# A two-layer attention block on one core: rotations, score products and VectorE's steps in another order

## What is computed

```python
proj = x @ w_in
a_in, b_in, c_in = jnp.split(proj, [A_COLS, A_COLS + B_COLS], axis=-1)
o_a = dilated_mixture(...)                       # 6 heads, kind "a"
o_b = diff_attention(bq[..., 0, :], bq[..., 1, :], bk[..., 0, :], bk[..., 1, :], bv, lam, ...)
                                                 # 4 heads, kind "b": a = probs(q1, k1) - lam * probs(q2, k2)
q = (rms_norm(c_q, ...) @ w_uq)                  # 6 heads, kind "c", from a latent
kv = (rms_norm(c_kv, ...) @ w_ukv)
q_c = concat([q[..., :C_NOPE], apply_rope(q[..., C_NOPE:])])
k_c = concat([kv[..., :C_NOPE], apply_rope(k_r)])
o_c = causal_attention(q_c, k_c, kv[..., C_NOPE:])
heads = jnp.concatenate([o_a, o_b, o_c], axis=-1)
h = layer_norm(DEEPNORM_ALPHA * x + heads @ w_o, ...)
```

## Time and profile before

| | us |
|---|---|
| median of 3 runs | 1985.44 (1985.15 to 1985.68) |
| the profiled execution | 1987.52 |
| its span, first to last instruction | 1985.6 |
| attention steps of the first of the two layers | about 841.8 to 937.4 |
| attention steps of the second | 628.6 later, about 1470.5 to 1566.0 |

### The profile page before, as it was taken

How to read it: one execution, slowest core, us unless ns; L and a number is a source line. 1 busy time by engine, 2 the same in 40 slices (tenths; PEclk the granted TensorE clock), 3 DMA queues, 4 the chain that set the end, 5 groups by cost and what they waited for, 6 DMA issues and landing times.

```text
span 1985.6 us, 26901 instructions
## 1 busy us (share of the span) xinstructions
PE 1934.6 (97%) x10454; PEld 1636.5 (82%) x10454; DVE 797.2 (40%) x1819; ACT 833.3 (42%) x1586; POOL 701.1 (35%) x553
## 2 busy tenths in 40 slices
PE   8999999999999999999999999999999999999997
PEld 4898889877789888877888888888887898888886
DVE  3665557442556435476511111017367551111003
ACT  3321268355237546577233232115477533232222
POOL 0523312125450335310544454445321245454542
PEclk9999999999999999999999999999999999999999
DMA  9544311112330124310333333222420123333321
GB/s 276 163 165 155 127 55 44 33 43 85 106 128 22 57 64 130 89 54 22 85 98 93 106 86 127 95 89 85 128 80 23 59 70 106 105 86 106 113 100 43
DMA packets 198261, 183.72 MB, mean 93 GB/s; under 512 B 31702, under 2 KB 166220, under 8 KB 198136
## 3 DMA queue, kind: packets, MB, share of 16 engines
q1 hardware_dynamic: 192104, 170.67, 27.9%
q10 hardware_dynamic: 6032, 11.33, 1.8%
HBM read 179.86 MB, written 5.40 MB: 93 GB/s over the span
## 4 chain that ended last, share of the span: by engine, by line
PE 86%; DVE 5%; ACT 3%; issue 2%; POOL 2%; DMA 1%; SPq 0%; DVEq 0%; ACTq 0%
PE ps L1330 23%; PE ps L1332 23%; PE ps L1331 23%; PE ps L1423 3%; PE ps L1918 2%; PE ps L1841 2%; POOL w_lo L731 2%; PE ps L1390 2%; PE ps L1409 2%; PE ps L1936 1%; PE ps L1453 1%; ACT w_hi L786 1%; PE ps L1368 1%; DVE sc L2498 1%; PE ps L1351 1%
## 5 line engine op out<-in xcount | busy, mean ns | idle before, releaser
L731 POOL TENSOR_TENSOR w_lo<-raw,w_hi 128x512 fp32r<-128x512 f32 (+1 forms) x518 | 679.2, 1343 | 1183.0 <-ACT w_hi L786 1182.9
L786 ACT ACTIVATE w_hi<-raw 128x1024 fp32r<-128x1024 f32 (+2 forms) x261 | 258.6, 1037 | 269.2 <-PE ps L1332 204.5
L1330 PE MATMUL ps<-g_hi,w_lo 128*128 128x512 f32 (+1 forms) x928 | 348.4, 375 | 1.4 <-POOL w_lo L731 1.4
L1331 PE MATMUL ps<-g_lo,w_hi 128*128 128x512 f32 (+1 forms) x928 | 347.5, 374 | 0.0
L1332 PE MATMUL ps<-g_hi,w_hi 128*128 128x512 f32 (+1 forms) x928 | 347.5, 374 | 0.0
L1330 PEld LDWEIGHTS ps<-g_hi,w_lo 128*128 128x128 f32 x928 | 174.7, 188 | 33.8 <-issue 1.7
L1331 PEld LDWEIGHTS ps<-g_lo,w_hi 128*128 128x128 f32 x928 | 174.7, 188 | 31.2
L1332 PEld LDWEIGHTS ps<-g_hi,w_hi 128*128 128x128 f32 x928 | 174.7, 188 | 30.9
L1330 PE MATMUL ps<-h_hi,w_lo 128*128 128x512 f32 (+1 forms) x496 | 180.1, 363 | 2.5 <-POOL w_lo L731 1.6
L2636 DVE TENSOR_TENSOR tmp_f<-ps,tmp_f 128x512 f32<-128x512 f32 x44 | 30.4, 692 | 370.7 <-PE ps L1332 370.7
L1331 PE MATMUL ps<-h_lo,w_hi 128*128 128x512 f32 (+1 forms) x496 | 174.6, 352 | 0.0
(11 more groups left out here) (293 smaller groups left out, 3469.3 us busy)
## 6 DMA issues: line engine op xcount, KB each, us to landing
raw<-in_w_in SPq DMA_DIRECT2D x30, 1024.0 KB, 5.1
raw<-in_w_mod SPq DMA_DIRECT2D x24, 1024.0 KB, 6.3
raw<-in_w_gate SPq DMA_DIRECT2D x44, 512.0 KB, 3.9
raw<-in_w_up SPq DMA_DIRECT2D x44, 512.0 KB, 5.1
raw<-in_w_down SPq DMA_DIRECT2D x22, 1024.0 KB, 4.8
raw<-in_w_out SPq DMA_DIRECT2D x8, 1024.0 KB, 5.0
strips<-bias_rows ACTq DMA_DIRECT2D x18, 256.0 KB, 3.5
raw<-in_w_in SPq DMA_DIRECT2D x16, 256.0 KB, 4.4
```

What stands on the lines that cost most here:

```text
L731: pool.tensor_tensor(w_lo[:, i % SPLIT, a:e], raw_of(what)[:, a:e], w_hi[:, i % SPLIT, a:e].bitcast(F32), ALU.subtract).then_inc(s_tile_lo ...
L786: act.activation(w_hi[:, i % SPLIT, a:b], raw_of(what)[:, a:b], ACT.Copy).then_inc(s_tile_hi.sem, s_tile_hi.nth((what, n)))
L1330: pe.matmul(o, lhs[1], rhs[0], start=first, stop=False)
L1331: pe.matmul(o, lhs[0], rhs[1], start=False, stop=False)
```

## The change

PE: the first rotation now stands behind the second key product instead of behind all three, the second behind the third. Scores 8 and 9 stand before the value products and not behind them. Score 10 stays behind them.

ACT: exp2(8) and exp2(9) come first, then the copies of the first three value products, then the copy of turn 0, then the copy of the fourth value product.

DVE: in each step the output rows come first, then the pair, then the scores, where it was scores, pair, rows.

The banks of the scores are shifted by one place, so that scores 8 and 9 go into banks 0 and 4, and the buffers are counted from unit 8, so that these two lie over the query weights, which are used up by then.

```diff
--- before.py
+++ after.py
@@ -602,7 +602,7 @@
             return u, ranks
 
         N_S, N_T, N_B, N_P = 3, 5, 5, 3
-        S_BANKS, T_BANKS = (0, 4, 6), (2, 1, 3, 5, 7)
+        S_BANKS, T_BANKS = (4, 6, 0), (2, 1, 3, 5, 7)
         UNITS, RANKS = units2()
         STEPS = len(UNITS) + N_B - 1
         FROM = N_B
@@ -610,7 +610,7 @@
 
         def probs_of(i):
 
-            return strips[:, B_HEADS + EARLY_AT[i], :] if i < EARLY else sc2[i % N_B]
+            return strips[:, B_HEADS + EARLY_AT[i], :] if i < EARLY else sc2[(i - EARLY) % N_B]
 
         LAST = len(RANKS) - 1
 
@@ -1232,9 +1232,15 @@
                         act.wait_ge(s_mm.sem, s_mm.at((y, what, c)))
                         for g in range(2):
                             act.activation(dst[0:HD, 2 * c + g, :], ps[HD * g:HD * g + HD, CB[what][c], :], ACT.Copy, scale=scale).then_inc(s_proj.sem, s_proj.nth((y, what, c, g)))
-                act.wait_ge(s_mm.sem, s_mm.at((y, "vc", XT - 1)))
-                for t in range(XT):
+                def vc_out(t):
+
+                    act.wait_ge(s_mm.sem, s_mm.at((y, "vc", t)))
                     act.activation(vc[:, t, :], ps[:, VCB[t], 0:384], ACT.Copy).then_inc(s_proj.sem, s_proj.nth((y, "vc", t)))
+
+                exp2(EARLY)
+                exp2(EARLY + 1)
+                for t in range(XT - 1):
+                    vc_out(t)
                 for step in range(FROM, STEPS):
                     r = turns(step)
                     if r is not None:
@@ -1243,7 +1249,9 @@
                         if r >= N_P:
                             act.wait_ge(s_mixed.sem, s_mixed.at((y, r - N_P)))
                         act.activation(pt2[r % N_P][:, 0:n], ps[:, TURNED["unit", r], 0:n], ACT.Copy).then_inc(s_pt.sem, s_pt.nth((y, r)))
-                    if EARLY <= step < len(UNITS):
+                    if step == FROM:
+                        vc_out(XT - 1)
+                    if EARLY + 2 <= step < len(UNITS):
                         exp2(step)
                     if LOADS_FROM <= step < LOADS_FROM + A_HEADS:
                         load_strip(step - LOADS_FROM, s_strips)
@@ -1873,6 +1881,13 @@
 
                 for g, n in ((0, P), (1, HD)):
                     up_q(4 * g, P * g, n, ("qr", g)).then_inc(s_mm.sem, s_mm.nth((y, "qr", g)))
+                def turn_rope(g, n):
+
+                    pe.wait_ge(*emptied[ROTB[g]])
+                    emptied[ROTB[g]] = s_roped.after((y, g))
+                    pe.wait_ge(s_proj.sem, s_proj.at((y, "qr", g)))
+                    pe.matmul(ps[0:n, ROTB[g], :], rot[0:n, 0:n], qr[0:n, g, :], start=True, stop=True).then_inc(s_rot.sem, s_rot.nth((y, g)))
+
                 for c in range(3):
                     b = CB["kn"][c]
                     pe.wait_ge(*emptied[b])
@@ -1880,13 +1895,12 @@
                     need((y, "up"), 2 * C_HEADS * QC + C_HEADS * HD)
                     mm3(ps[:, b, :], both_parts(ukv, lambda r: r[:, P * c:P * c + P]), both_parts(CKV, lambda r: r[:]),
                         True, True).then_inc(s_mm.sem, s_mm.nth((y, "kn", c)))
-                for g, n in ((0, P), (1, QC)):
-                    pe.wait_ge(*emptied[ROTB[g]])
-                    emptied[ROTB[g]] = s_roped.after((y, g))
-                    pe.wait_ge(s_proj.sem, s_proj.at((y, "qr", g)))
-                    pe.matmul(ps[0:n, ROTB[g], :], rot[0:n, 0:n], qr[0:n, g, :], start=True, stop=True).then_inc(s_rot.sem, s_rot.nth((y, g)))
+                    if c > 0:
+                        turn_rope(*((0, P), (1, QC))[c - 1])
                 for c in range(3):
                     up_q(CB["qn"][c], C_HEADS * ROPE + P * c, P, ("qn", c, 1)).then_inc(s_mm.sem, s_mm.nth((y, "qn", c)))
+                for i in range(EARLY, EARLY + 2):
+                    score(i)
                 for t in range(XT):
                     b = VCB[t]
                     pe.wait_ge(*emptied[b])
@@ -1918,7 +1932,7 @@
                         m = pe.matmul(ps[:, b, 0:HD], pt2[r % N_P][:, P * j:P * j + P], v, start=j == 0, stop=j == len(u["vs"]) - 1)
                     m.then_inc(s_mixed.sem, s_mixed.nth((y, r)))
 
-                for i in range(EARLY, EARLY + N_S):
+                for i in range(EARLY + 2, EARLY + N_S):
                     score(i)
                 for step in range(FROM, STEPS):
                     if EARLY + N_S <= step < len(UNITS):
@@ -2561,6 +2575,10 @@
                                     ALU.mult).then_inc(s_o_out.sem, s_o_out.nth((y, r)))
 
                 for st in range(EARLY, STEPS):
+                    if turns(st) is not None and turns(st) >= 3:
+                        rows_out2(turns(st) - 3)
+                    if EARLY <= st - 2 < len(UNITS) and UNITS[st - 2]["second"]:
+                        pair(st - 2)
                     if st < len(UNITS):
                         u = UNITS[st]
                         if st >= EARLY + N_B and UNITS[st - N_B]["first"]:
@@ -2572,10 +2590,6 @@
                         if u["kind"] == "a":
                             dve.wait_ge(s_strips.sem, s_strips.at(y))
                         scored(st)
-                    if EARLY <= st - 2 < len(UNITS) and UNITS[st - 2]["second"]:
-                        pair(st - 2)
-                    if turns(st) is not None and turns(st) >= 3:
-                        rows_out2(turns(st) - 3)
                     sub_norm(st)
                     if st - 2 in turn_at:
                         k = turn_at[st - 2]
```

## The result

The changed kernel takes 1996.52 us (median of 5 runs, 1991.77 to 2003.41) against 1985.15 us before (5 runs, 1984.20 to 1985.68): a ratio of 1.0062 with a 95% interval of 1.0051 to 1.0072. It is slower by 0.6%, where I had forecast 1978.8 and a range from 1974.5 to 1984.5. The profiled execution took 2003.41 us for a span of 2001.6, and its TensorE clock over the whole span was 0.985 of full; the four other runs had 0.984 to 0.991.

A forecast was written before the change was run, and what follows sets the result against it. The prediction took PE, busy 88.09 of 94.20 us in the first layer's attention, as the bound. Start +0.35, pairs -2.3 and rows -1.3 made -3.3 a layer, -6.6 in all: 1978.8 us, range 1974.5 to 1984.5.

The forecast's parts named there:

- Start of the steps: +0.35 us a layer: Start of attention steps: rope 0.68 earlier, but turn 0 waits for ACT's delayed value copy; +0.35 us a layer.
- +1.5 if the 1.7 us passed on in full: Upper bound for the start of the attention steps, if PE's stand ahead of turn 0 delayed everything behind it.
- The turn of 848.69: Early PE turn waiting for pair(9), 848.69 in the trace before; forecast at 849.05.
- hidden exponentials: Lower bound for the start of the attention steps: ACT's exponentials hidden, the rope's 0.68 us won; -0.7 a layer.
- Pairs, -2.3: DVE's pairs ahead of scores in the attention steps shorten PE's waits: -2.3 us a layer, bounds 0 and -4.
- rows, -1.3: DVE's output rows first in the attention steps shorten PE's waits for banks: -1.3 us a layer, bounds -0.3 and -1.9.
- What would show it: Profile signs: PE's pair and row waits under 2.5 us, DVE waiting for exponentials, score 10 to last mix 3-4 us shorter.
- Rival 2: Attention steps: pair at DVE's head waits for its exponential, delaying scores and PE; +3.5 us a layer, 1992.4; chance 0.08.
- Rival 1: Attention gain mostly given back through a dearer start or ACT's delayed exponentials: 1981.5 to 1985 us; chance 0.24.
- Rival 3: In each layer a DVE pair meets GpSimd's weight split: 0.7 us a layer worse than forecast, 1980.2; chance 0.05.
- Rival 4: All PE waits in the attention steps but the start's go: 5 us a layer, 1975.4; chance 0.08.

The follow-up runs named there:

- the stand filled: Changed kernel plus seven matmuls of ones on TensorE between score 10 and turn 0 in each layer: 1980.95 us, ratio 0.9981.
- the copies first: Changed kernel with ScalarE making all four value copies before exp2(8) and exp2(9): 1977.15 us, ratio 0.9959.
- the second stand filled: Kernel before with VectorE's new order, plus four matmuls of ones ahead of the turn of the first second head: 1978.96 us, ratio 0.9967.
- the put-in stand: Kernel before with five more ScalarE copies ahead of the four value copies, so that turn 0 starts later: 2005.04 us, ratio 1.0103.
- the front alone: Changed kernel with VectorE's old order and the old place of the rotations: 2008.38 us, ratio 1.0121.
- the first place filled: Kernel before with five more ScalarE copies ahead of the value copies, plus seven matmuls of ones ahead of turn 0: 1997.99 us, ratio 1.0076.
- the upper group: Kernel before with VectorE's new order alone: seven of 12 runs at 1988.50 to 1991.40 us; the other five at 1978.39 to 1981.45.

## Why the prediction was wrong, point by point

**The step that failed** is the price of the stand ahead of turn 0, in "Start of the steps: +0.35 us a layer". The prediction saw the stand: "PE stands about 1.7 us where it stood not at all". It priced it at its own length, carried that through to the next turn, and gave "+1.5 if the 1.7 us passed on in full" as the upper bound. It had read that "PE's granted clock is 1.00 in all four stretches", and then took every PE duration of the earlier trace rows as given, whatever stands were put among them. What the runs showed in its place: with the stand the clock falls, and the fall costs 10.65 us a layer in the profiled execution; the other runs of the changed kernel, at a clock of up to 0.991, paid less, down to about the price of one such fall in all. The four stretches read for the prediction have no half clock, but the rest of the same trace has it, at 436.7 and at 726.9, each time behind a stand of PE. So the risk could be read there. Its size could not: those two falls last 3.4 us, those in the attention steps 17 to 38 us. A bound could have been worked out: PE at half clock for the work of even ten microseconds costs more than the whole gain forecast, and that case should have stood among the rivals with a chance.

**The timing of the start was near, apart from the clock.** I count from the start of the last query product (839.51 before, 837.51 after). The rope's first operation came 0.70 us earlier against it (forecast 0.7). The stand was 1.74 us, put down to ACT's value copy (forecast about 1.7). Mix 0 came at +7.18 (forecast 846.45, so +6.94; before +5.94). The turn of 848.69, before at +9.18, was forecast at +9.54 and came at +9.90 with the stand filled, and at +10.31 in the changed kernel, already at half clock. So at full clock the start costs 0.72 us against the +9.18 of before, where +0.35 was forecast. With the copies first the same turn comes at +8.47 (845.09 and 836.62), 0.71 earlier than before, which is the lower bound that the prediction gave for hidden exponentials (-0.7).

**Pairs, -2.3: too much by themselves; rows, -1.3: right.** Alone they gave some 0.8 (1.7 us over two layers) and 1.3. The prediction counted three waits for rows "just behind a pair" as gains of the pair's move. They stay until the rows move as well. Together the two gave 3.1 a layer (1978.96 against 1985.16, with the second stand filled) of 3.6 forecast, so the sum was near and its split was not.

**What would show it.** Waits for pairs and rows are 2.3 us with the stand filled (0.9 and 1.4), as forecast under 2.5; the 1.6 of the changed kernel itself is partly a matter of its slow PE. DVE's wait for score products fell from 15.4 us to 6.4 with the stand filled, but its head then waited mostly for the mixes that its rows need (7.3 us), not for exponentials as forecast. From score 10 to the last mix the kernel with the copies first takes 89.69 us (839.65 to 929.34), 3.2 less than the 92.84 of before (843.23 to 936.07), as forecast; filled it takes 91.12; the changed kernel 101.77.

**The rivals.** Rival 2 had the sign of the result and another mechanism. It did not happen: DVE's waits for exponentials in the changed kernel, 841.84 to 939, are these two, of which the first belongs to the sums of the rows, and they are as small at full clock, with the stand filled:

```profile
DVE recips L2572 <- ACT sc L1213: 1.2, 1, 1.2
DVE small L2520 <- ACT sc L1213: 1.1, 2, 0.8
```

Rival 1 said that the start would give the gain back through ACT; the place was right and the size out by a factor of seven. Its upper end was also added up wrongly: +1.5, -1.1 and -1.3 give -0.9 a layer, not -0.3. Rival 3 did not happen in the first layer: the changed kernel's pairs of 384 columns take 0.62 us there. Rival 4 decided nothing.

**The sum, mended**, for one layer: start with its stand +0.72, pairs and rows -3.1, fall of the clock +10.65 where it happens, together +8.3; the profiled layer lost 8.2. With the stand taken away, the start is -0.71 and the sum -3.8, and the layer of copies first takes 92.72 us (836.62 to 929.34) where before takes 96.56. The whole kernel with copies first measured -8.4 us against 1985.51; the forecast for the whole change was -6.6.

## What to carry to other kernels

A new stand of PE of 1 to 2 us can cost six times its length through the clock (10.65 us for 1.74, among turns, mixes and scores), so it belongs among the rivals with that price, and the granted clock behind it is the first thing to read in the result, ahead of the waits. Read the clock over the whole trace of before too: a short fall elsewhere shows that stands of this length can do it. The head of an engine's queue belongs to work whose inputs are there already: the place of four value copies decided between 1996.5 and 1977.2 us. Where two things release one wait, move both, since moving one hands the wait to the other.

## What the runs showed of the hardware

- TensorE's clock fell from 1.00 to 0.50 around the end of a stand: 1.8 us after PE had begun again in the changed kernel (843.37 and 845.2), 2.2 us after it in the kernel with the put-in stand (842.17 and 844.4), but 0.3 us before it in the second layer of the front alone (1484.87 and 1484.6). It stayed there for 23.9 us in the changed kernel although PE was busy for 22.00 of 22.00 us in that time. In other executions it lasted about 17 us (the put-in stand with the first place filled, 847.6 to 864.7), about 20 and 27 us (the front alone) and about 37.5 us (the put-in stand, 844.4 to 881.9).
- In the kernel before the clock fell twice for 3.4 us, behind stands of 2.85 and 1.37 us (and once more at its end, where PE has no work left). In the first case PE was busy for 3.40 of 3.40 us at half clock, with products of 512 columns. Another stand of 1.25 us (ahead of 718.89) left it at 1.00. Why it came back after 3.4 us there and after 17 to 38 us in the attention steps, no run tests.
- In the attention steps the fall was seen at stands of 1.74, 1.75, 0.97 (with 0.26 behind it) and 1.24 us. The stand of 1.24 us is in the kernel before too; there one of the 70 runs that show a clock had a lower one (0.992, 1997.06 us). With VectorE's new order it was 7 of 12 runs, with five copies ahead and the first place filled all 6 (0.984 to 0.993), of which one, profiled, shows the fall at that stand. What tips it is open: I have no profiled execution of the upper group, and in the lower one PE's row up to the stand is that of before: the turn behind it starts 9.19 us after the last query product (848.90 and 839.71), before 9.18.
- The Trainium skill, "TensorE: Matmul & The Clock Gate", section "A second HAM failure mode: psum-queue depth-cycling", tells of a kernel in which PE idles so briefly and so often between groups of matmuls that its clock swings between half and full. The traces here agree in that stands of 0.97 to 1.75 us were enough; they differ in that one stand did it, and the clock then stayed at half for 17 us and more instead of swinging.
